# Seven products of sums in place of eight, in the branch projections and the output projection of a hybrid decoder layer

## The chip, the cores and the metric

The kernel runs on one core of a Trainium2 chip. The metric is the device time of one execution in microseconds, the median of three runs. TensorE multiplies float32r operands here, each split into a high and a low part, so every product of matrices is made of three matmuls: high by high, high by low and low by high.

## The reference, cut to what matters

A layer with two parallel branches works on 2048 prompt tokens and 8 sample tokens, with D_MODEL = 1024:

```python
xn = rmsnorm(x, norm_w)
proj = xn @ w_in                      # q k v i f o z_m b c x_c z_c g_m g_c, 10,248 columns
h, C1, n1, m1 = mlstm_chunkwise(q, k, v, ig, lf, ...)
h = h * rsqrt(mean(h * h) + EPS) * head_norm_w
y_m = (h * sigmoid(o_pre) * silu(z_m)) @ w_proj_m
cv, conv1 = short_conv(c_g * x_c, conv0, conv_w)
y_c = (silu(z_c) * b_g * cv) @ w_proj_c
mix = sigmoid(g_m) * y_m + sigmoid(g_c) * y_c
out = x + mix @ w_out
y = rmsnorm(out, final_norm_w)
```

The three products with `w_proj_m`, `w_proj_c` and `w_out` (1024 x 1024 each) are what the change is about.

## The kernel before

The kernel has four phases, one after another, with a barrier of all engines between them.

Phase A norms the input and computes the `v` columns.

Phase B is the input projection for the other columns. It goes over the tokens in three passes of 688, 688 and 680. In a pass it takes 36 pairs of weight column blocks (128 columns each); 18 bodies of two pairs make up the first pass, called `qk` (2), `oz` (4), `conv` (8) and `gates` (4) by what they compute. For each pair the four quarters of the problem (two halves of K by two halves of the tokens by two column blocks) are computed with seven products of sums in the place of eight plain ones, by Winograd's scheme (seven products, fifteen sums). VectorE (DVE) makes the sums of the weights in pass 0 (`sums`), SyncE (SP) stores them to `w_ops_d` and later passes load them. ScalarE (ACT) makes the high part of each operand (`w_high`), DVE the low part (`w_low`), and DVE adds the products up as they leave PSUM (`step`). In passes 1 and 2 the recurrence of the mLSTM is computed between the products. `body` in each engine's program is one such body; all engines go through them in the same order, and each engine's queue is in order. SP issues all DMAs: in a body it loads the weights of the pairs two and three ahead (`load_w`), and stores finished rows (`store_rows`) and sums (`store_w`). GpSimd (POOL) does little: the sums of the x operands at the turn of a pass (`x_sums`, `x_difference`, `x_late`) and small powers.

Phase C computes the branch projections plainly. It keeps `w_proj_m` and `w_proj_c`, split in high and low, in SBUF (`RH`, `RL`) and goes over 7 tiles of TN = 294 tokens; for each of two branches and 8 output blocks it issues 8 x 3 matmuls of 294 columns (line 2017). DVE multiplies the PSUM results by the gates (`gate_m`, `gate_c`) and a tile of `mix` is stored to DRAM.

Phase D loads `w_out` over the same buffers and goes over 17 tiles of 128 tokens (the last has 8); each takes 2 x 8 x 3 matmuls of 512 columns with the activations as the stationary operand (line 2207). DVE adds the residual, ACT squares, POOL takes the power, DVE scales by `final_norm_w`, and SP stores.

Of the kernel before, what the change touches and what calls it, by code (L numbers as in the profile page):

```python
# [28 lines left out]
P = 128  # L29
# [20 lines left out]
TN = 294  # L50
NTC = 7
TP = TN * NTC
# [31 lines left out]

class Shared:
# [3 lines left out]
def build(nc, inputs, outputs):  # L89
# [4 lines left out]
    with top:  # L94
# [9 lines left out]
        g.w_ops_d = dram("w_ops_d", NPP, P, 4 * 4 * P)  # L104
        g.qT_d = dram("qT_d", NH, P, TP)
# [14 lines left out]
        g.stage_in = {name: [top.enter_context(nc.semaphore(f"{name}_in{j}")) for j in range(2)] for name in ("wc", "mix")}  # L120
        g.mix_out = top.enter_context(nc.semaphore("mix_out"))
# [3 lines left out]
        g.act_in = top.enter_context(nc.semaphore("act_in"))  # L125
# [3 lines left out]
        g.XS = sbuf(nc, early, "x_quarters", [P, 5, 4, TQ])  # L129
        g.LH = sbuf(nc, early, "w_hi", [P, NOP, 4, P], F32R)  # L130
        g.LL = sbuf(nc, early, "w_lo", [P, NOP, 4, P], F32R)
        g.X0H = sbuf(nc, early, "x_hi0", [P, 4, TQ], F32R)
# [3 lines left out]
        g.v_stored = [early.enter_context(nc.semaphore(f"a_v_stored{j}")) for j in range(2)]  # L136
        with early:
            phase_a(nc, g)
            phase_b(nc, g)
        g.RH = sbuf(nc, top, "RH", [P, KB, 2 * D], F32R)  # L140
        g.RL = sbuf(nc, top, "RL", [P, KB, 2 * D], F32R)
        g.A0 = [sbuf(nc, top, f"first_act_{n}", [P, KB, TN], F32R) for n in ("hi", "lo")]
        g.m_hi, g.m_ready = top.enter_context(nc.semaphore("m_hi")), top.enter_context(nc.semaphore("m_ready"))
        g.RHf = g.RH[:, :, :].bitcast(F32)
        phase_c(nc, g)
        phase_d(nc, g)

# [469 lines left out]
def phase_b(nc, g):  # L617
# [54 lines left out]
    BANK = (0, 1, 2, 3, 0, 2, 3)  # L672
# [16 lines left out]
    const_in, const_set, pads = sem("const_in"), sem("const_set"), sem("pads")  # L689
    kq_in, m_in, v_in, gate_in, hg_out = sem("kq_in"), sem("m_in"), sem("v_in"), sem("gate_in"), sem("hg_out")  # L690
# [36 lines left out]
    def over_segments(eng, body):  # L727
# [11 lines left out]
        return before  # L739

# [66 lines left out]
    with nc.Block() as block:  # L807
# [3 lines left out]
        def _(sp):  # L811
# [40 lines left out]

            def store_w(pair, par):
# [133 lines left out]
            def body(p, s, i, extra, following, before):  # L987
# [19 lines left out]
                if s == "gates" and i == 0 and p < 2:  # L1007
                    load_quarters(p + 1)
# [1237 lines left out]
```

## Time and profile before

| | |
|---|---|
| device time, three runs | 2356.53, 2359.93, 2360.93 us; median 2359.93 |
| span of the profiled execution | 2356.7 us; the page has no other time for it |
| TensorE (PE) busy | 2323.1 us, 99% of the span, 14,643 matmuls |
| VectorE busy | 1488.1 us, 63% |
| ScalarE busy | 948.6 us, 40% |
| GpSimd busy | 77.5 us, 3% |
| DMA | 425.66 MB, mean 181 GB/s |

The profile's line numbers (L1658) are those of the kernel file. A row of the timeline gives the start, the time taken, the engine, the line and the operation, and in square brackets how long the engine had been idle and what released it. Instructions in a row overlap by some 0.08 us on VectorE, so their starts stand closer than their durations. For TensorE a matmul's duration is the time until its result is out; the rate is given by the distance of the starts.

### The profile page before, as it was taken

The page shows a single profiled execution, that of the slowest core. Times are in us where ns is not written, and L with a number is a line of the kernel's source. Part 1 is how long each engine was busy: PE and PEld are TensorE (multiplying, and loading weights), DVE is VectorE, ACT ScalarE, POOL GpSimd, SP SyncE. Part 2 cuts the span into 40 slices and gives each one's busy share as a digit, 9 for nine tenths or more (in the row PEclk, how much of TensorE's full clock was granted, in tenths as well). Part 3 has the DMA queues.
Part 4 walks back from the last instruction along what each step waited for, and adds up shares of the span by engine and source line. Part 5 has one row for each costly group of instructions (what it writes and reads, how often), then busy time and mean ns, then how long its engine had stood idle before and what let it go on. Part 6 is the DMA issues. An engine that isn't in the chain of part 4 may idle for free. (4 is left out here: it accounts for less than half of the span.)

```text
span 2356.7 us, 41040 instructions
## 1 busy us (share of the span) xinstructions
PE 2323.1 (99%) x14643; PEld 2254.8 (96%) x14643; DVE 1488.1 (63%) x2703; ACT 948.6 (40%) x1717; POOL 77.5 (3%) x84
## 2 busy tenths in 40 slices
PE   8999999999999999999999999999999999999998
PEld 8998999999999999999999999999998999998886
DVE  4447788898876687777776677777755333324333
ACT  3224444444454444455655444555554101002121
POOL 0011000000110000000020000000000000000000
PEclk9999999999999999999999999999999999999999
DMA  6665655455775765656765766557567433443442
GB/s 224 209 215 136 199 187 181 157 177 176 232 220 174 232 202 184 191 159 195 240 191 177 235 202 195 188 175 217 176 185 260 156 102 110 138 143 126 138 138 86
DMA packets 424977, 425.66 MB, mean 181 GB/s; under 512 B 32810, under 2 KB 363690, under 8 KB 424870
## 3 DMA queue, kind: packets, MB, share of 16 engines
q1 hardware_dynamic: 424870, 424.25, 56.9%
q8 instruction: 66, 1.08, 0.2%
q14 instruction: 41, 0.34, 0.0%
HBM read 297.36 MB, written 126.85 MB: 180 GB/s over the span
## 5 line engine op out<-in xcount | busy, mean ns | idle before, releaser
L1658 PE MATMUL b_g<-x_hi,w_hi 128*128 128x344 f32 (+1 forms) x3024 | 985.5, 326 | 9.0 <-DVE rows L1333 4.3
L1658 PE MATMUL b_g<-x_lo,w_hi 128*128 128x344 f32 (+1 forms) x3024 | 967.9, 320 | 0.0
L1658 PE MATMUL b_g<-x_hi,w_lo 128*128 128x344 f32 (+1 forms) x3024 | 967.0, 320 | 0.0
L1658 PEld LDWEIGHTS b_g<-x_hi,w_hi 128*128 128x128 f32 x3024 | 569.3, 188 | 16.1 <-DVE rows L1333 4.4
L1658 PEld LDWEIGHTS b_g<-x_lo,w_hi 128*128 128x128 f32 x3024 | 569.3, 188 | 1.7
L1658 PEld LDWEIGHTS b_g<-x_hi,w_lo 128*128 128x128 f32 x3024 | 569.4, 188 | 0.0
L1155 ACT ACTIVATE w_hi<-w_operands 128x512 fp32r<-128x512 f32 x519 | 323.5, 628 | 272.9 <-PE b_g L1658 261.2
L1295 DVE TENSOR_TENSOR w_lo<-w_operands,w_hi 128x512 fp32r<-128x512 f32 x519 | 354.2, 695 | 1.2
L1155 ACT ACTIVATE w_hi<-stages 128x512 fp32r<-128x512 f32 x216 | 134.7, 629 | 138.3 <-PE b_g L1658 119.4
L1295 DVE TENSOR_TENSOR w_lo<-stages,w_hi 128x512 fp32r<-128x512 f32 x216 | 145.6, 684 | 7.7 <-ACT w_hi L1155 6.9
L2017 PE MATMUL c_g<-act_hi,RH 128*128 128x294 f32 x448 | 134.4, 300 | 2.1 <-DVE rows L1948 2.1
L2017 PE MATMUL c_g<-first_act_hi,RH 128*128 128x294 f32 x448 | 134.1, 299 | 1.6 <-DVE RL L1941 1.6
L2017 PE MATMUL c_g<-act_hi,RL 128*128 128x294 f32 x448 | 134.0, 299 | 0.0
L2017 PE MATMUL c_g<-first_act_hi,RL 128*128 128x294 f32 x448 | 133.8, 299 | 0.0
L2017 PE MATMUL c_g<-first_act_lo,RH 128*128 128x294 f32 x448 | 133.7, 299 | 0.0
L2017 PE MATMUL c_g<-act_lo,RH 128*128 128x294 f32 x448 | 133.5, 298 | 0.0
L579 PE MATMUL a_v<-wv_hi,xT_hi 128*128 128x344 f32 (+1 forms) x384 | 124.5, 324 | 4.5 <-DVE wv_lo L481 2.8
L1326 DVE TENSOR_TENSOR part<-part,b_g 128x344 f32<-128x344 f32 (+1 forms) x108 | 55.1, 510 | 112.4 <-PE b_g L1658 112.0
L579 PE MATMUL a_v<-wv_lo,xT_hi 128*128 128x344 f32 (+1 forms) x384 | 122.7, 320 | 0.0
L579 PE MATMUL a_v<-wv_hi,xT_lo 128*128 128x344 f32 (+1 forms) x384 | 122.7, 319 | 0.0
L1335 DVE TENSOR_TENSOR rows<-part,b_g 128x344 f32<-128x344 f32 (+1 forms) x108 | 55.1, 510 | 89.8 <-PE b_g L1658 87.9
L1173 ACT ACTIVATE part<-b_g 128x344 f32<-128x344 f32 (+1 forms) x108 | 49.3, 457 | 143.5 <-PE b_g L1658 143.4
(305 smaller groups left out, 3116.0 us busy)
## 6 DMA issues: line engine op xcount, KB each, us to landing
w_operands<-w_in SPq DMA_DIRECT2D x282, 256.0 KB, 5.2
stages<-w_ops_d SPq DMA_DIRECT2D x36, 768.0 KB, 5.5
w_operands<-w_ops_d SPq DMA_DIRECT2D x34, 768.0 KB, 4.9
stages<-w_in SPq DMA_DIRECT2D x72, 256.0 KB, 3.8
w_operands<-w_ops_d SPq DMA_DIRECT2D x70, 256.0 KB, 6.3
w_ops_d<-w_operands SPq DMA_DIRECT2D x18, 768.0 KB, 3.3
w_ops_d<-stages SPq DMA_DIRECT2D x18, 768.0 KB, 3.4
w_ops_d<-w_operands SPq DMA_DIRECT2D x36, 256.0 KB, 3.9
```

The source lines that it names most:

```text
L579: last = nc.tensor.matmul(V[3 * (i % 2) + j][:n, 0:VC], x[:, k, 0:n], w[:, k, j * VC:(j + 1) * VC], start=(k == 0 and m == 0), stop=(k == ...
L1155: nc.scalar.activation(LH[:, j], operand(g, par, j), ACT.Copy).then_inc(w_hi, 1)
L1173: nc.scalar.activation(P1[:, 0:n], G[0][:, 0:n], ACT.Copy).then_inc(x_free, 1)
L1295: nc.vector.tensor_tensor(LL[:, j], operand(g, par, j), LH[:, j].bitcast(F32), ALU.subtract).then_inc(w_ready, 1)
L1326: nc.vector.tensor_tensor(U2[:, 0:n], P1[:, 0:n], G[1][:, 0:n], ALU.add).then_inc(ev, 1)
L1335: nc.vector.tensor_tensor(ER[:, q, 1, 0:n], U2[:, 0:n], G[2][:, 0:n], ALU.add).then_inc(ev, 1)
L1658: last = nc.tensor.matmul(bank[:, 0:n], w[:, j, k, :], x[:, k, 0:n], start=(j < 4 and k == 0 and m == 0), stop=(k == 3 and m == 2), skip_g ...
L2017: last = nc.tensor.matmul(G[o % NB][:, 0:TN], w[:, k, c0:c0 + P], x[:, k, :], start=(k == 0 and m == 0), stop=(k == KB - 1 and m == 2))
```

## The change

Phases C and D become one phase, `phase_cd`, without a barrier between them, in which both the branch projections and the output projection use the seven-product scheme of phase B.

- **Branches.** Tokens go in 4 groups of 2 x 258 (TN = 258, NG = 4). For each branch, group and pair of output blocks there are 7 products of 4 x 3 matmuls of 258 columns. Two column pairs are interleaved in a unit `u`, so 16 units of 14 products. ACT copies the first and the fifth product of each out of PSUM, DVE adds the other five (`step`), and a gate is one operation over 1032 columns (`gate`).
- **Output.** Tiles of 2 x 128 tokens, 8 of them, each 7 products of 4 x 3 matmuls of 512 columns; the 8 sample rows come last with 48 plain matmuls.
- **Merge of the branches.** `mix_d` gets the first branch's rows by a plain store, and the second branch's by 16 accumulating DMAs that GpSimd issues (`accumulate`).
- **Weights.** The 12 pairs of weight blocks (4 for each matrix) are read in 12 bodies of the first pass of phase B (`block_of`: `oz` 1 to 3, all of `conv`, `gates` 0). GpSimd makes four sums for each (`projection_sum`), and all seven operands are kept in `proj_d` in DRAM. The buffers used (`kT`, `qT`, `MB` and `HB`) are not otherwise in use then. The operands are loaded in phase CD, seven at a time, and split there in high and low by ACT and DVE.
- **head_norm_w** is no longer folded into `w_proj_m` but into the `z` rows: ACT has one more operation of 688 columns for each `oz` row.
- The sums of the activations (`act_sum`) and their splits (`act_high`, `act_low`) are made once for four column pairs. The first group's are made in the last bodies of phase B.

The diff, cut to its core:

```diff
-TN = 294
-NTC = 7
-TP = TN * NTC
+TN = 258
+NG = 4
+TP = 2 * TN * NG
+NU = 4 * NG
...
+            def load_weights(b):
+                if b:
+                    sp.wait_ge(q_out, 16 * NOP * b)
+                w, c0, c1 = weight_block(g, b)
+                w = w[0].rearrange("(k p) n -> p k n", p=P)
+                for place, k0, c in zip(raw_pieces, (0, 0, 4, 4), (c0, c1, c0, c1)):
+                    sp.dma_start(place, w[:, k0:k0 + 4, c:c + P]).then_inc(q_in, 16)
+                for j, k0, c in ((0, 0, c0), (4, 4, c0), (5, 4, c1)):
+                    sp.dma_start(g.proj_d[b, :, j], w[:, k0:k0 + 4, c:c + P]).then_inc(q_out, 16)
+            def store_sums(b):
+                sp.wait_ge(q_set, 4 * (b + 1))
+                for place, j in zip(raw_pieces[1:], (2, 6, 1, 3)):
+                    sp.dma_start(g.proj_d[b, :, j], place).then_inc(q_out, 16)
...
+                if block_of(p, s, i) is not None:
+                    load_weights(block_of(p, s, i))
                 if extra == "dec_inputs":
                     decode_inputs()
                 if extra == "dec_rows":
                     decode_rows()
...
+            def projection_sum(b, at):
+                r0, r1, r2, r3, t = raw_pieces
+                if at == 0:
+                    pool.wait_ge(q_in, 64 * (b + 1))
+                    nc.gpsimd.tensor_tensor(t, r1, r3, ALU.add).then_inc(q_set, 1)
+                elif at == 1:
+                    pool.wait_ge(q_set, 4 * b + 1)
+                    nc.gpsimd.tensor_tensor(r3, t, r0, ALU.subtract).then_inc(q_set, 1)
+                elif at == 2:
+                    nc.gpsimd.tensor_tensor(r1, r0, r1, ALU.subtract).then_inc(q_set, 1)
+                else:
+                    pool.wait_ge(q_set, 4 * b + 2)
+                    nc.gpsimd.tensor_tensor(r2, r2, r3, ALU.subtract).then_inc(q_set, 1)
...
+def act_low(nc, dve, g, s, j):
+    high, low = act_parts(g, s, j)
+    dve.wait_ge(g.x_hi, 7 * s + j + 1)
+    nc.vector.tensor_tensor(low, act_source(g, s, j), high.bitcast(F32), ALU.subtract).then_inc(g.x_ready, 1)
...
+            def accumulate(n):
+                pool.wait_ge(gated, n + 1)
+                pool.dma_start(two_rows(g.mix_d, n), MX[n % 2], accum_op=ALU.add).then_inc(g.acc_out[n % 2], 16)
...
+            for u in range(NU):
+                s = u // 2 + 1
+                for j in range(NOP):
+                    if j == 0 and u:
+                        gate(2 * u - 2)
+                        gate(2 * u - 1)
+                        if u % 2 == 0:
+                            act_low(nc, dve, g, s - 1, NOP - 1)
+                    step(2 * u, j)
+                    step(2 * u + 1, j)
+                    if u == 0 and 1 <= j < 4:
+                        split_low(nc, dve, g, 0, j + 3)
+                        act_low(nc, dve, g, 0, j + 3)
+                        split_low(nc, dve, g, 1, j + 3)
+                    for b, o in behind(u, j):
+                        split_low(nc, dve, g, b, o)
+                    if u % 2 == 0 and j >= 5:
+                        act_sum(nc, dve, g, s, j - 5)
+                    if u % 2 and j:
+                        act_low(nc, dve, g, s, j - 1)
+                        if j < 3:
+                            act_sum(nc, dve, g, s, j + 1)
...
+            def branch_product(n, j):
+                br, t, p = place(n)
+                if t == 0:
+                    pe.wait_ge(g.w_ready, split_count(4 * br + p, j))
+                if p == 0:
+                    pe.wait_ge(g.x_ready, 7 * (n // 4) + j + 1)
+                if n > 1:
+                    bank_free(n - 2, j, copies, parts_made)
+                bank_read(n, j, copies, parts_made)
+                high, low = act_parts(g, n // 4, j)
+                bank = G[4 * (n % 2) + BANK[j]]
+                for k in range(4):
+                    for m, (w, x) in enumerate(((0, high), (0, low), (1, high))):
+                        last = nc.tensor.matmul(bank[:, 0:TN], g.W[:, p, j, w, k, :], x[:, k, :], ...)
```

SyncE's queue in the `oz` bodies of the first pass, before (the loads into `stages` are the weights of the pair three ahead, those into `w_operands` x4 of the pair two ahead; `gate_d` is a finished row, `w_ops_d` the sums of phase B):

```order
L162 DMA w_operands<-w_in 128x4x128 [waits b_w_ops_out0,b_w_ready]
L162 DMA w_operands<-w_in 128x4x128 x3
L863 DMA gate_d<-rows 128x680 [waits b_gate_set]
L865 DMA gate_d<-rows 128x8
L857 DMA w_ops_d<-stages 128x1536 [waits b_w_sums_set]
L858 DMA w_ops_d<-w_operands 128x512
L162 DMA stages<-w_in 128x4x128 [waits b_w_ops_out1,b_w_ready]
```

And the same stretch in the changed kernel:

```order
L207 DMA w_operands<-w_in 128x4x128 [waits b_w_ops_out0,b_w_ready]
L207 DMA w_operands<-w_in 128x4x128 x3
L1044 DMA gate_d<-rows 128x680 [waits b_gate_set]
L1046 DMA gate_d<-rows 128x8
L1038 DMA w_ops_d<-stages 128x1536 [waits b_w_sums_set]
L1039 DMA w_ops_d<-w_operands 128x512
L1025 DMA kT<-w_proj_m 128x4x128 [waits b_q_out]
L1025 DMA qT<-w_proj_m 128x4x128
L1025 DMA neg_max<-w_proj_m 128x4x128
L1025 DMA h<-w_proj_m 128x4x128
L1027 DMA proj_d<-w_proj_m 128x4x128 x3
L207 DMA stages<-w_in 128x4x128 [waits b_w_ops_out1,b_w_ready]
```

Seven DMAs, with a wait for the stores of the block before, stand ahead of the load of the pair three ahead. At the body's end, ahead of the next body's load of the pair two ahead, stand the four stores of sums (`proj_d` from `qT`, `neg_max` and twice `h`), the first of which waits for GpSimd's sums.

GpSimd's queue in the first pass, before: after the constants only loop branches stand ahead of the sums at the turn of the pass.

```order
L1132 AFFINE_SELECT cum_upper<-ones 128x128 [waits b_const_set]
L1134 AFFINE_SELECT mask<-mask 128x128
L736 UNCONDITIONAL_BRANCH
L736 REGISTER_ALU
L736 COMPARE_AND_BRANCH
L736 UNCONDITIONAL_BRANCH
```

In the changed kernel, at the same place, the first loop has the four sums of a block (`h`, `qT`, `kT` and `neg_max` are the borrowed buffers):

```order
L1347 AFFINE_SELECT mask<-mask 128x128
L893 UNCONDITIONAL_BRANCH
L893 ISA
L1309 TENSOR_TENSOR h<-qT,h 128x512 [waits b_q_in]
L1311 ISA
L1312 TENSOR_TENSOR h<-h,kT 128x512 [waits b_q_set]
L1314 TENSOR_TENSOR qT<-kT,qT 128x512
L1316 REGISTER_ALU
L1317 TENSOR_TENSOR neg_max<-neg_max,h 128x512 [waits b_q_set]
```

Each of the four reads two SBUF tensors of 512 columns; they run twelve times in all. VectorE's program in that pass is as before.

VectorE's queue near the start of phase C, before (`RL` are low parts of weights, `act_lo` of activations; `rows` takes results out of PSUM, with the gate):

```order
L1941 SCALAR_TENSOR_TENSOR RL<-stages,head_norm_q,RH 128x1024 [waits c_w_hi]
L1941 SCALAR_TENSOR_TENSOR RL<-act_stage,head_norm_q,RH 128x1024 [waits c_w_hi]
L1935 TENSOR_TENSOR act_lo<-act_stage,act_hi 128x2352 [waits c_a_hi1]
L1944 TENSOR_TENSOR RL<-act_stage,RH 128x1024 [waits c_w_hi]
L1948 SCALAR_TENSOR_TENSOR rows<-tanh_gate,c_g 128x294 [waits last_rows_out1,c_tile_done,last_rows_out0,c_tg_in0]
L1948 SCALAR_TENSOR_TENSOR rows<-tanh_gate,c_g 128x294 [waits c_tile_done] x2
L1944 TENSOR_TENSOR RL<-stages,RH 128x1024 [waits c_w_hi]
L1948 SCALAR_TENSOR_TENSOR rows<-tanh_gate,c_g 128x294 [waits c_tile_done] x3
```

And in the first unit of the new phase (`proj_whole` are weight operands as loaded, `proj_ops` their parts; `c_part` and `rows` take sums out of PSUM):

```order
L319 TENSOR_TENSOR act_lo_b<-x_quarters,act_hi_b 128x1032 [waits xq_hi]
L242 TENSOR_TENSOR proj_ops<-proj_whole_55,proj_ops 128x512 [waits proj_hi]
L242 TENSOR_TENSOR proj_ops<-proj_whole_56,proj_ops 128x512 [waits proj_hi]
L242 TENSOR_TENSOR proj_ops<-proj_whole_57,proj_ops 128x512 [waits proj_hi]
L2303 TENSOR_TENSOR rows<-c_part,c_g 128x258 [waits c_done] x2
L242 TENSOR_TENSOR proj_ops<-proj_whole_56,proj_ops 128x512 [waits proj_hi]
L242 TENSOR_TENSOR proj_ops<-proj_whole_57,proj_ops 128x512 [waits proj_hi]
L273 TENSOR_TENSOR x_quarters<-x_quarters 128x1032 [waits xq_in1]
L2306 TENSOR_TENSOR rows<-c_part,c_g 128x258 [waits c_done] x2
L242 TENSOR_TENSOR proj_ops<-proj_whole_56,proj_ops 128x512 [waits proj_hi]
L242 TENSOR_TENSOR proj_ops<-proj_whole_57,proj_ops 128x512 [waits proj_hi]
L276 TENSOR_TENSOR x_quarters<-x_quarters 128x1032 [waits xq_sum]
```

Here the first sum for the second group of activations (`x_quarters`, waiting for `xq_in1`, its load) stands ahead of the reads of PSUM for the seventh product (L2306) and of later weight parts.

## Rows read from the trace of the kernel before

**Rows 1.** The page: busy time, share of the span, instructions.
```profile
PE 2323.1 (99%) x14643; PEld 2254.8 (96%) x14643; DVE 1488.1 (63%) x2703; ACT 948.6 (40%) x1717; POOL 77.5 (3%) x84
```

**Rows 2.** Stretches: length, then busy us (count) by engine, granted clock, DMA share, GB/s.
```profile
358.73:385.28 26.55, 26.55 (x170) 26.55 (x170) 21.31 (x37) 12.77 (x24) 0.00 (x0) 1.00 0.56 185
518.03:544.58 26.55, 26.55 (x170) 26.55 (x169) 23.62 (x43) 11.67 (x20) 0.00 (x0) 1.00 0.52 171
597.68:624.23 26.55, 26.55 (x170) 26.55 (x169) 20.73 (x36) 12.24 (x21) 1.04 (x1) 1.00 0.84 278
1830.00:2150.00 320.00, 320.00 (x2354) 320.00 (x2353) 108.72 (x173) 35.16 (x21) 0.00 (x0) 1.00 0.39 125
2173.00:2340.00 167.00, 167.00 (x720) 134.62 (x720) 56.86 (x75) 30.55 (x45) 8.13 (x15) 1.00 0.43 132
```

**Rows 3.** TensorE's timeline at the borders of phases C and D, and its last matmul.
```profile
1783.50 2.02 PE L2023 MATMUL c_g<-ident 128*128 128x128 f32 x16 [0.87 <-PEq L807]
1786.42 0.37 PE L2017 MATMUL c_g<-first_act_hi,RH 128*128 128x294 f32 x1 [0.90 <-DVE RL L1941]
...
2156.22 0.29 PE L2017 MATMUL c_g<-act_hi,RL 128*128 128x294 f32 x1
2158.39 0.47 PE L2207 MATMUL d_g<-RH,first_act_hi 128*128 128x512 f32 x1 [1.87 <-PEq L1814]
...
2349.41 0.40 PE L2207 MATMUL d_g<-RH,first_act_lo 128*8 128x512 f32 x1
```

**Rows 4.** TensorE's timeline in phase B: eight records of 128 columns in a row.
```profile
1004.28 1.04 PE L1717 MATMUL b_t<-ident,h 128*128 128x128 f32 x8
1005.07 0.40 PE L1658 MATMUL b_g<-x_hi,w_hi 128*128 128x344 f32 x1
```

**Rows 5.** GpSimd's timeline: sums of 512 and of 1376 columns.
```profile
172.49 1.29 POOL L363 TENSOR_TENSOR w_operands<-w_operands 128x512 f32<-128x512 f32 x1
...
626.81 3.50 POOL L1095 TENSOR_TENSOR x_quarters<-x_quarters 128x1376 f32<-128x1376 f32 x1
697.24 3.17 POOL L1101 TENSOR_TENSOR x_quarters<-x_quarters 128x1376 f32<-128x1376 f32 x1 [66.92 <-DVE x_lo L1316]
```

**Rows 6.** VectorE's timeline at the same times.
```profile
623.03 0.69 DVE L1295 TENSOR_TENSOR w_lo<-w_operands,w_hi 128x512 fp32r<-128x512 f32 x1
626.29 0.99 DVE L1302 TENSOR_TENSOR stages<-stages,w_operands 128x512 f32<-128x512 f32 x1 [2.58 <-DMA w_operands<-w_in]
627.21 0.50 DVE L1337 TENSOR_TENSOR rows<-part,b_g 128x344 f32<-128x344 f32 x1
627.63 3.23 DVE L1295 TENSOR_TENSOR w_lo<-w_operands,w_hi 128x512 fp32r<-128x512 f32 x1
...
695.57 1.59 DVE L1316 TENSOR_TENSOR x_lo<-x_quarters,x_hi 128x1376 fp32r<-128x1376 f32 x1
697.50 4.35 DVE L1316 TENSOR_TENSOR x_lo<-x_quarters,x_hi 128x1376 fp32r<-128x1376 f32 x1
```

**Rows 7.** SyncE's issues in a `conv` body.
```profile
530.21 0.46 SPq L858 DMA_DIRECT2D w_ops_d<-w_operands  x1
534.13 0.38 SPq L162 DMA_DIRECT2D stages<-w_in  x1
534.55 0.51 SPq L162 DMA_DIRECT2D w_operands<-w_in  x1
```

**Rows 8.** SyncE and VectorE in `conv` 2: rows sent through DRAM.
```profile
451.74 0.81 SPq L970 DMA_DIRECT2D qk_rows<-scores  x1
...
458.43 0.44 SPq L977 DMA_DIRECT2D sample_wide<-fir_d  x1
...
462.13 0.23 DVE L1570 TENSOR_TENSOR sample_wide<-sample_wide 128x64 f32<-128x64 f32 x1 [3.40 <-DMA sample_wide<-fir_d]
```

**Rows 9.** DMA issues by tile: count, KB each, median us to landing.
```profile
w_operands<-w_in SPq DMA_DIRECT2D x282, 256.0 KB, 5.2
...
mix_d<-rows SPq DMA_DIRECT2D x7, 1176.0 KB, 6.7
```

More of the change, by code:

```diff
@@ L1113, in body @@
             def body(p, s, i, extra, before):
+                if block_of(p, s, i) is not None:
+                    for at in range(4):
+                        projection_sum(block_of(p, s, i), at)
                 if extra == "chunk":
@@ new lines, in phase_cd @@
+    N = D // 2
+    at = g.places
+    tail = g.XS[:, :, :, :].rearrange("p s k n -> p (s k n)")[:, 20 * TN:26 * TN].rearrange("p (a n) -> p a n", n=TN)
+    TG = [at_place(nc, "tanh_gate", [P, 2, 2 * TN], at["gate"])[:, :, :], tail[:, 0:4].rearrange("p (a h) n -> p a (h n)", a=2)]
+    P1 = [tail[:, 4], tail[:, 5]]
+    parts = at_place(nc, "c_part", [P, 2, TN], at["part"])
+    U2 = [parts[:, 0], parts[:, 1]]
+    rows = g.ER[:, :, :, :].rearrange("p q r n -> p q (r n)")
+    MX = [rows[:, q, 0:4 * TN].rearrange("p (a n) -> p a n", a=2) for q in range(2)]
@@ new lines, in y_stored, with two_rows, row_free, behind @@
+    def y_stored(i):
+        return 16 * (NU // 2 + i // 2 + 1)
+    def two_rows(a, n):
+        _, t, p = place(n)
+        return a.rearrange("(a b) p n -> b p a n", a=2)[p][:, :, t * 2 * TN:(t + 1) * 2 * TN]
+    def row_free(eng, n):
+        if n < 2:
+            eng.wait_ge(g.row_out[n], g.rows_stored[n])
+        elif n - 2 < NU:
+            eng.wait_ge(rows_out[n % 2], 16 * ((n - 2) // 2 + 1))
+        else:
+            eng.wait_ge(g.acc_out[n % 2], 16 * ((n - 2 - NU) // 2 + 1))
+    def behind(u, j):
+        found = split_behind(u, j)
+        return [(2 * found[0] + q, found[1]) for q in range(2)] if found else []
@@ L1914, in _ @@
+            act_high(nc, act, g, 0, 3)
             for br in range(2):
                 row = g.ER[:, 1, br, 0:2 * PASSES[2][1]]
[L1916 to L1925 removed]
@@ new lines, in _ @@
+            pe.wait_ge(sx_set, 3)
+            pe.wait_ge(copied, out_copies(NT2 - 2, 4))
+            pe.wait_ge(ev, out_parts(NT2 - 2, 1))
+            for h, operands in enumerate((((0, 0), (1, 4)), ((0, 3), (2, 5)))):
+                count = 0
+                for a, j in operands:
+                    for k in range(4):
+                        for x, w in ((SH, 0), (SH, 1), (SL, 0)):
+                            last = nc.tensor.matmul(G[h][:NS, :], x[:, a, k, :], g.W[:, :, j, w, k, :],
+                                                    start=(count == 0), stop=(count == 23))
+                            count += 1
```

906 lines of the change are left out of this document (513 added, 393 removed).

## The prediction

> **What bounds the kernel now.** First the busy times of the page [rows 1]: TensorE is busy for 2323.1 of 2356.7 us, so only fewer or shorter matmuls, or fewer gaps between them, can give much. Next the stretches by engine [rows 2]. The reader should divide length by count there. In phase B 170 records (344 columns for nearly all) take 26.55 us, 156.2 ns each. In phase C 2354 matmuls of 294 columns take 320 us, 135.9 ns. In phase D 720 of 512 columns take 167 us, 231.9 ns. TensorE has no gap in these stretches and the granted clock is 1.00, so each is at the rate of TensorE itself. Last the borders [rows 3]: phase C's first TensorE work starts at 1783.50, phase D's at 2158.39, the last matmul ends at 2349.8, and 6.9 us of norm and store follow.
>
> **What the change takes off TensorE.** The branches have 2 x 8 x 7 tiles x 24 = 2688 matmuls of 294 columns now, and 32 x 7 x 12 = 2688 of 258 columns after. The count stays; seven products for eight shows as narrower matmuls (2064 x 7/8 columns and padding). From 344 to 294 columns the spacing falls by 20.3 ns, 0.41 ns a column; from 512 to 344 by 0.45 [rows 2]. For 36 columns fewer than 294 that gives 119.7 to 121.3 ns; I take 121. Sum: 2688 x 0.121 = 325.2 us. The output has 17 x 48 = 816 matmuls of 512 columns now and 8 x 84 + 48 = 720 after: 720 x 0.2319 = 167.0 us.
>
> Now the two phases take 2158.39 - 1783.50 = 374.9 us (with 16 ident records, the waits at the start and the barrier to D) and 2349.8 - 2158.4 = 191.4 us [rows 3]. If the new phase starts at once and never waits, it needs 492.2 in place of 566.3: **74.1 us less**. The end is the same chain for the 8 sample rows, 6.9 us.
>
> **What it adds in the first pass.** Twelve bodies get four GpSimd sums of 512 columns. One takes 1.29 us [rows 5], so 5.2 us a body. They are not free for VectorE. Read [rows 5] and [rows 6] side by side: while GpSimd runs its sum from 626.81 to 630.31, a `w_lo` of VectorE that takes 0.69 otherwise takes 3.23, and ends 0.55 after GpSimd. `x_lo` takes 1.59 alone and 4.35 beside the sum of 697.24. A sum out of PSUM (0.50 at 627.21) isn't held up. So an operation of VectorE with both inputs in SBUF waits for the whole GpSimd sum. The Trainium skill, "SBUF — State Buffer", "Who interferes with whom", says the same as a rule: the two engines take a shared read port by an exclusive lock for the whole instruction. By that rule "sums on GpSimd" would cost VectorE all of its 5.2 us; the trace agrees.
>
> VectorE's room in a body is 26.55 less its busy time [rows 2]: 5.2 us in `oz`, 2.9 in `conv`, 5.8 in `gates`. Of the 5.2 us some part is no loss, since a PSUM read (0.42 from start to start, 627.21 to 627.63) can run under a sum; with one under every second sum 4.3 us are lost. Then `oz` and `gates` still fit, and each of the 8 `conv` bodies is 1.4 us over: 11 us. Bounds: nothing, if TensorE's slack in PSUM banks (a bank is read two products after its result, 3.8 us) hides it; 2.3 x 8 = 18 us, if all 5.2 are lost.
>
> SyncE has seven more issues ahead of the load of the pair three ahead. At 0.42 to 0.55 us each these take 3.7 us; the gap there is 3.5 (530.67 to 534.13) [rows 7]. That is hidden, and so are the four stores at the body's end. The added traffic is 11 x 256 KB = 2.9 MB a body, on top of 171 GB/s x 26.55 us = 4.5 MB: 280 GB/s. The busiest stretch shown moved 278 GB/s at a DMA share of 0.84 [rows 2], without a TensorE gap. So `conv` and `oz` are near the limit but under it; `gates` 0 is that very stretch and goes to 385 GB/s. I put 2 us on it. One place is worse: in `conv` 2, `load_weights` stands ahead of `decode_rows`. Now SyncE goes from 451.74 to 458.43 through it, the broadcast lands at 462.1, and VectorE has already waited 3.40 us [rows 8]. 3.7 us of issues and the queued 1.8 MB (5 to 6 us at 330 GB/s, which is 278 at a share of 0.84 taken to the full [rows 2]) come in front: VectorE waits some 5 us longer. TensorE has to pay most of that, 4 us. Sum for the pass: 11 + 4 + 2 = **17 us**, bounds 3 and 35 (upper: 18, and late weight loads costing up to 2 us a `conv` body with the DMA queue full).
>
> ACT's added operation on `z` rows (688 columns) lies in bodies where ACT is busy for 12.8 of 26.55 us [rows 2]: nothing.
>
> **What it adds in the new phase.** A unit `u` is 168 matmuls, 20.3 us. VectorE's work in it, from start-to-start times: a sum out of PSUM 0.42 at 344 columns, 0.34 at 258 (less 86 columns at 1.05 ns, the slope from 512 to 1376 columns, 0.69 to 1.59 us [rows 6]); a split or sum of 1032 columns 1.15; a weight split 0.60. An even unit has 10 x 0.34 + 2 gates + 1 + 2 x 1.15 = 9.2 us, an odd one 10 x 0.34 + 10 x 1.15 = 14.9. Unit 0 has no gates, but ten weight splits with four activation splits, six weight splits of the next pair and two sums: 3.4 + 9.6 + 4.6 + 2.3 = 19.9. Unit 1 has eight more weight splits, 19.7. Elsewhere it is at most 18. So VectorE is full only for the first two units, and there it stands at the sum that waits for `xq_in1`: that load is issued when the first group is split (some 16 us into the phase), is 2.1 MB behind 4 MB of weights and gates, and lands about 25 us in, 5 to 6 us after VectorE is there. The weight parts for unit 1 behind it then come 1 to 2 us late in three places: **5 us**, bounds 1 and 15. In the output part VectorE has 5 x 0.64 + 7 x 0.60 + 4 x 0.60 + 4 x 1.15 = 14.4 us of 19.5 for a tile: 0.5 us.
>
> The accumulating DMAs (528 KB) have no row. The nearest is a store of 1176 KB with 6.7 us to landing [rows 9], and a load of 256 KB with 5.2; for 528 KB I take 6 to 10. The rows are written again 7.7 us after the second gate, and 5.8 us more pass before TensorE needs that bank. So it costs nothing up to 13 us of latency, and its upper bound is in the rivals.
>
> **Sum**: 2356.7 - 74.1 + 17 + 5.5 = 2305.1. The median of the runs is 3.2 us above the profiled span, so the median after is **2308 us**.
>
> **The rivals.**
> - *The first pass hides it all* (chance 0.22). For it: most of VectorE's delay is under the bank slack, and `conv` has idle of its own. Pass cost 3, new phase 1 to 5: 2359.9 - 74.1 + 4 to 8, 2290 to 2294.
> - *The first pass is paced by VectorE and DMA* (0.15). For it: [rows 6], and 280 GB/s through one queue with 512-byte pieces. Cost 35 to 50 us: 2326 to 2341.
> - *The weight load paces TensorE* (0.04), so that 258 columns go no faster than 294: 40 us dearer, 2348. For it: the weight loader is busy for 320.00 of 320 us in C [rows 2]. Against: its time shrinks with the columns, and eight records of 128 columns start within 0.79 us, 110 ns each or less [rows 4].
> - *Slower than before* (0.05): the accumulating DMA takes so long that ACT and VectorE stand at `row_free`. From 13 us on, each us costs a us in each of 7 units; the 52 us of the sum are eaten at 13 + 7.5, some 20 us latency; at 22 it gives 2371. For it: an accumulation reads and writes DRAM, and GpSimd must write its descriptors. Against: 1176 KB land in 6.7 us.
> - *The seven products don't save*: in the branches the count stays at 2688, and if the rate per column were not kept (a gap at each of 224 + 56 product changes, each with up to four waits, of 0.1 us) it would cost 28 us: 2336 (0.04). Phase B has the same changes with 0 gaps.
>
> **How the numbers follow.** The forecast's own case (2298 to 2324) has 0.50. 80% range: from 2286 (the first rival inside) to 2334 (the upper part of the second outside). Below 0.2% (4.7 us) this kernel's runs can't tell a change. Faster 0.93, same 0.02, slower 0.05.
>
> **What would show it.** Right: matmuls of 258 columns 121 ns apart; no 2 us gap before the 512-column ones; `w_lo` rows of 1.5 to 2 us beside GpSimd's sums and TensorE gaps of 1 to 2 us in the `conv` bodies, a longer one in `conv` 2; a gap or two in units 0 and 1. Wrong: TensorE without gaps in pass 0 (then some 2290), or gaps in every unit from the second branch on, with `row_free` or `acc_out` behind them (then over 2330).

## The result and the profile after

The changed kernel takes **2377.8 us** (four runs, 2374.4 to 2378.8), the kernel before 2360.3 beside it. The ratio is 1.0077, with a 95% interval of 1.0063 to 1.0092: **slower by 0.8%**, where 2% faster was forecast, and far outside the range. The profiled execution took 2374.4, its span is 2372.4 us.

The page of the changed kernel: busy times, and the queue that GpSimd's DMAs use (packets, MB, share).

```profile
PE 2283.7 (96%) x14531; PEld 2209.3 (93%) x14531; DVE 1690.8 (71%) x2947; ACT 1059.2 (45%) x1961; POOL 166.2 (7%) x140
...
q0 software_dynamic: 4352, 8.46, 2.3%
```

Against [rows 1], TensorE is busy for 39 us less and yet the span is 16 us longer: it now idles for 89 us, not 34. The stretches show where. First the kernel before (phase B), then the changed kernel: phase B, branches, output, one `conv` body, and 60 us in the middle of the branches. The columns are those of [rows 2].

```profile
216.00:1782.60 1566.60, 1558.39 (x9833) 1540.06 (x9833) 1180.36 (x2162) 789.13 (x1521) 52.59 (x33) 1.00 0.62 193
```

```profile
217.00:1816.00 1599.00, 1567.18 (x9833) 1542.26 (x9833) 1227.65 (x2171) 810.33 (x1552) 125.22 (x85) 0.99 0.68 213
1818.00:2194.50 376.50, 340.33 (x2688) 337.78 (x2689) 232.44 (x344) 120.10 (x197) 17.19 (x15) 0.95 0.65 185
2195.00:2365.00 170.00, 168.76 (x719) 129.61 (x718) 124.04 (x179) 60.17 (x107) 8.00 (x10) 1.00 0.47 145
...
560.53:588.55 28.02, 27.54 (x170) 26.46 (x168) 27.20 (x43) 11.55 (x21) 5.92 (x4) 1.00 0.84 266
...
1900.00:1960.00 60.00, 60.00 (x502) 60.00 (x501) 37.07 (x52) 15.10 (x23) 0.00 (x0) 1.00 0.48 150
```

The gain is real where nothing waits: 502 matmuls of 258 columns in 60 us are 119.5 ns each. At that rate the branches would take 2688 x 0.1195 = 321 us. They take 376.5: 36 us more in which TensorE is idle, and 19 more in which it is busy but slow (mean granted clock 0.95). The output takes 170, as forecast to 3 us. Phase B is 32 us longer, some 25 of them in its first pass (run 7 has the rows for this).

**The gaps of the branches.** TensorE's timeline has pauses of 3.75, 3.12, 1.22, 5.30, 4.80 and 7.24 us in units 9 to 15, nearly one in each unit. The timeline around the last one, of GpSimd, VectorE, ACT and TensorE:

```profile
2171.61 1.20 POOL L2185 DMA_DIRECT2D mix_d<-rows  x1 [19.53 <-DVE rows L2312]
...
2181.36 0.42 DVE L2300 TENSOR_TENSOR rows<-rows,c_g 128x258 f32<-128x258 f32 x1 [1.36 <-DMA mix_d<-rows]
...
2181.57 1.22 POOL L2185 DMA_DIRECT2D mix_d<-rows  x1 [8.76 <-issue]
...
2191.29 0.39 ACT L2222 ACTIVATE rows<-c_g 128x258 f32<-128x258 f32 x1 [7.19 <-DMA mix_d<-rows]
2191.33 0.42 DVE L2300 TENSOR_TENSOR rows<-rows,c_g 128x258 f32<-128x258 f32 x1 [9.55 <-DMA mix_d<-rows]
...
2191.81 0.58 PE L2458 MATMUL c_g<-act_hi_b,proj_ops 128*128 128x258 f32 x1 [7.24 <-DVE rows L2300]
...
2193.91 0.42 PE L2458 MATMUL c_g<-act_hi_b,proj_ops 128*128 128x258 f32 x1
2194.12 0.42 PE L2458 MATMUL c_g<-act_lo_b,proj_ops 128*128 128x258 f32 x1
```

Read from the end: TensorE waits for VectorE's step, that for the buffer of the second gated row, and that for its accumulating DMA. The two rows of a unit are gated 1.2 us apart, but GpSimd issues the second DMA 10 us after the first. It lands 9.6 us after that, 19.6 us after the first issue and 18.8 after its own row was gated. The last two rows show the other cost: behind the pause the matmuls stand 0.21 us apart, not 0.12, and the next row of the windows gives the granted clock there.

```profile
2192.40:2194.50 2.10, 2.10 (x11) 2.10 (x11) 2.10 (x4) 2.10 (x5) 0.00 (x0) 0.50 0.00 0
```

0.50 is the level of 1.2 GHz. And GpSimd's second issue comes at 2181.57, just as the first DMA has landed and released VectorE (2181.36). The line L2185 as a group: who waited for it (us, times), and its time to landing.

```profile
  DVE rows L2300: 71.0, 13
  ACT rows L2222: 63.6, 9
...
DMA to landing us min/median/max: 6.0/8.4/10.2
```

**The gaps of the first pass.** `conv` 2 and the first `gates` body, SyncE's issues first.

```profile
454.52 0.94 SPq L1025 DMA_DIRECT2D kT<-w_proj_c  x1
...
461.04 0.86 SPq L1151 DMA_DIRECT2D qk_rows<-scores  x1
...
470.72 0.23 DVE L1792 TENSOR_TENSOR sample_wide<-sample_wide 128x64 f32<-128x64 f32 x1 [9.19 <-DMA sample_wide<-fir_d]
...
471.63 0.62 PE L1889 MATMUL b_g<-x_hi,w_hi 128*128 128x344 f32 x1 [7.33 <-DVE rows L1555]
...
628.97 3.95 SPq L1133 DMA_DIRECT2D x_quarters<-xT_d  x4
632.96 1.10 SPq L1025 DMA_DIRECT2D kT<-w_out  x1
634.11 2.47 SPq L1025 DMA_DIRECT2D qT<-w_out  x1
...
643.94 0.58 SPq L207 DMA_DIRECT2D stages<-w_in  x1
...
650.93 3.26 DVE L1524 TENSOR_TENSOR stages<-stages,w_operands 128x512 f32<-128x512 f32 x1 [11.02 <-DMA w_operands<-w_in]
...
654.67 0.66 PE L1889 MATMUL b_g<-x_hi,w_hi 128*128 128x344 f32 x1 [8.31 <-DVE rows L1559]
```

The seven issues of a block take SyncE 6.5 us in `conv` 2 and 11.0 in the first `gates` body (632.96 to 643.94), not 3.7. VectorE waits 9.2 us for the broadcast (3.40 in [rows 8]) and 11.0 for weights of phase B. Both times TensorE pauses, and runs at the half level behind it.

### The profile page after: what moved, and what is told of

The parts are those of the page before. It is cut to its first block, busy times and chain, and to the rows that moved or that the text cites. A ratio compares the mean times of both kernels' runs of the same rounds, so it can differ in the third digit from the quotient of the medians.

```text
span 2372.4 us, 41561 instructions
## 1 busy us (share of the span) xinstructions
PE 2283.7 (96%) x14531; PEld 2209.3 (93%) x14531; DVE 1690.8 (71%) x2947; ACT 1059.2 (45%) x1961; POOL 166.2 (7%) x140
## 4 chain that ended last, share of the span: by engine, by line
PE 59%; DVE 12%; DMA 8%; issue 6%; SPq 3%; ACT 1%; DVEq 0%; POOL 0%; ACTq 0%; POOLq 0%
PE b_g L1889 44%; PE c_g L2458 5%; PE c_g L2482 5%; DMA mix_d<-rows 3%; DMA w_operands<-w_ops_d 2%; DVE w_lo L1517 2%; PE b_n L1943 1%; PE b_n L1944 1%; PE b_s L1942 1%; DVE proj_ops L242 1%; DMA proj_whole<-proj_d 1%; DMA new_C_sample<-gate 1%; DMA y_prompt<-y 1%; DVE x_lo L1538 1%; DVE act_lo_a L319 1%
## 5 line engine op out<-in xcount | busy, mean ns | idle before, releaser
L1889 PE MATMUL b_g<-x_hi,w_hi 128*128 128x344 f32 (+1 forms) x3024 | 988.4, 327 | 34.2 <-DVE rows L1555 14.5
L1517 DVE TENSOR_TENSOR w_lo<-w_operands,w_hi 128x512 fp32r<-128x512 f32 x519 | 368.8, 723 | 1.2
L2458 PE MATMUL c_g<-act_hi_a,proj_ops 128*128 128x258 f32 x1024 | 195.7, 291 | 8.6 <-DVE proj_ops L242 4.7
L2458 PE MATMUL c_g<-act_hi_b,proj_ops 128*128 128x258 f32 x768 | 149.2, 291 | 29.4 <-DVE rows L2300 26.6
L2458 PEld LDWEIGHTS c_g<-act_hi_a,proj_ops 128*128 128x128 f32 x1024 | 166.3, 197 | 9.6 <-DVE proj_ops L242 7.2
L2458 PEld LDWEIGHTS c_g<-act_hi_b,proj_ops 128*128 128x128 f32 x768 | 124.9, 196 | 31.2 <-DVE rows L2300 24.1
L2458 PE MATMUL c_g<-act_lo_a,proj_ops 128*128 128x258 f32 x512 | 148.3, 290 | 0.0
L2482 PE MATMUL c_g<-proj_ops,act_hi_a 128*128 128x512 f32 x448 | 141.4, 396 | 1.2 <-DVE y L2379 0.9
L313 ACT ACTIVATE act_hi_a<-x_quarters 128x512 fp32r<-128x512 f32 (+1 forms) x88 | 68.9, 786 | 95.8 <-PE c_g L2482 50.2
L2458 PE MATMUL c_g<-act_lo_b,proj_ops 128*128 128x258 f32 x384 | 111.2, 290 | 0.0
```

What stands on the lines that cost most here:

```text
L313: nc.scalar.activation(act_parts(g, s, j)[0], act_source(g, s, j), ACT.Copy).then_inc(g.x_hi, 1)
L1517: nc.vector.tensor_tensor(LL[:, j], operand(g, par, j), LH[:, j].bitcast(F32), ALU.subtract).then_inc(w_ready, 1)
L1889: last = nc.tensor.matmul(bank[:, 0:n], w[:, j, k, :], x[:, k, 0:n], start=(j < 4 and k == 0 and m == 0), stop=(k == 3 and m == 2), skip_g ...
L2458: last = nc.tensor.matmul(bank[:, 0:TN], g.W[:, p, j, w, k, :], x[:, k, :], start=(j < 4 and k == 0 and m == 0), stop=(k == 3 and m == 2), ...
L2482: last = nc.tensor.matmul(bank[:, :], x[:, k, :], g.W[:, :, j, w, k, :], start=(j < 4 and k == 0 and m == 0), stop=(k == 3 and m == 2), sk ...
```

## The experiments

Each ran beside the kernel before; "won" is the change of the ratio against that of the changed kernel (1.0077), times 2360 us.

**1. More descriptor space** (with the small tiles moved to make room):

```diff
-    nc = bacc.Bacc("TRN2", ..., dynamic_dma_scratch_size=1024)
+    nc = bacc.Bacc("TRN2", ..., dynamic_dma_scratch_size=3072)
```

> The computation is the changed kernel's; GpSimd's space for DMA descriptors is 3072 bytes in place of 1024, and small tiles moved elsewhere to make room. In the changed kernel the second accumulating DMA of a unit is issued 9.0 to 10.6 us after the first, each time 0.3 us after the first has landed, and the second's rows are free only some 18 us after their gate. Theory A (the descriptor space holds one of these DMAs, so the second waits for the first to land): the second issue follows within 3 us of the first, both rows are free 8 to 13 us after their gate, TensorE's gaps in units 8 to 15 (26 us, and 34 us of half clock behind them) shrink to under 6 us, and the time is 2374 - 35 = 2339 us (2330 to 2348). Theory B (GpSimd needs 9 us to write the descriptors of one, or an accumulation is slow in itself): the distance stays at 9 to 10 us and the time within 4 us of the changed kernel's.

2359.6 us, ratio 1.0004 (0.9995 to 1.0014): 17 us won. GpSimd's timeline and the landing time of its DMAs:

```profile
2159.04 2.44 POOL L2186 DMA_DIRECT2D mix_d<-rows  x2 [28.64 <-DVE rows L2313]
...
DMA to landing us min/median/max: 6.6/10.0/13.6
```

The second issue now follows the first at once, in all eight units. The serial issue of theory A is shown. Its sum isn't: the time is 12 us over the top of its range. Two DMAs in flight land later (10.0 us in the median, up to 13.6), and the rows still cost pauses of 0.5 to 2.2 us in units 9 to 15, 7.1 us together. And there is a gap of 7.2 us at 2150.6, with 10.2 us at the half level, that isn't the rows':

```profile
2129.89 13.41 SPq L266 DMA_DIRECT2D x_quarters<-mix_d  x8
...
2149.11 1.15 ACT L238 ACTIVATE proj_ops<-proj_whole 128x512 fp32r<-128x512 f32 x2 [23.50 <-DMA proj_whole<-proj_d]
```

ACT's copy of a product stands behind the split of an output weight, and SyncE issues that weight's load only behind 13.4 us of issues for the output's activations.

**2. No accumulation:** the second branch's rows go out through SyncE like the first's.

```diff
-                sp.dma_start(two_rows(g.mix_d, n), MX[n % 2]).then_inc(rows_out[n % 2], 16)
+                out = rows_out[n % 2] if n < NU else g.acc_out[n % 2]
+                sp.dma_start(two_rows(g.mix_d, n), MX[n % 2]).then_inc(out, 16)
```

> The second branch's rows are stored plainly by SyncE over the first branch's, without accumulation: the sum of the branches is left out. The bytes stored are the same, GpSimd issues no DMA. If the gaps of units 8 to 15 come from the accumulating DMAs (their serial issue or their slowness), they vanish as in units 1 to 6, where the same rows go out by plain stores that land in 8 to 9 us: 2374 - 40 = 2334 us (2326 to 2342). If they come from something else in those units (the loads of the third pair of weight blocks, the activations, VectorE's own work), the gaps stay and the time is within 5 us of 2374. Against the run with the larger descriptor space: equal within 5 us if only the serial issue cost time; lower by over 5 us if accumulation itself is slow too.

2344.2 us, 0.9938 (0.9921 to 0.9954): 33 us won, 2 us over the range expected; the branches take 341.4 us for 376.5. The gaps of units 8 to 15 are gone but one of 2.5 us, at the start of unit 15; those of units 1 and 7 stay. It is 15 us under run 1, so to issue the accumulating DMAs together won only half of what taking them away won. About half of the 15 are run 1's pauses for rows (7.1 us); most of the rest is its gap behind the output weights, 7.2 us there and 2.5 here, and the half level behind it. Whether accumulation as such makes that gap longer was not tried.

**3. Four buffers for the gated rows**, accumulation and descriptor space as in the changed kernel:

```diff
-    MX = [rows[:, q, 0:4 * TN].rearrange("p (a n) -> p a n", a=2) for q in range(2)]
+    MX = [r.rearrange("p (a n) -> p a n", a=2) for r in
+          (S_flat[:, 0:4 * TN], S_flat[:, 4 * TN:8 * TN], rows[:, 0, 0:4 * TN], rows[:, 1, 0:4 * TN])]
...
+        elif n - 4 < NU:
+            eng.wait_ge(mix_out[n % 4][0], mix_out[n % 4][1] + 16 * (n // 4))
+        else:
+            eng.wait_ge(g.acc_out[n % 4], 16 * ((n - 4 - NU) // 4 + 1))
```

> The computation is the changed kernel's, with the descriptor space of 1024 bytes; the gated rows of the new phase take turns in four buffers in place of two (the two new ones lie in the staging buffer, which is idle there), so that the rows of a unit are written again two units later. Theory (the rows come free too late: 18 us after the gate against a need after about 13): with a full unit of 20 us more, no wait for a store or an accumulating DMA is left in ACT or VectorE in units 2 to 15, the gaps of 26 us in units 8 to 15, the half clock behind them (34 us, worth 17) and the gap of 1.1 to 3 us at unit 8 go: 2378 - 40 = 2338 us (2330 to 2345). The run with more descriptor space gave 2360: if this one is equal to it, the waits for rows were not what cost the rest, and contention with the accumulating DMAs is.

2346.0 us, 0.9943 (0.9927 to 0.996): 32 us won, one us over the range expected. The branches:

```profile
1818.40:2162.90 344.50, 330.45 (x2688) 329.19 (x2689) 232.45 (x343) 118.45 (x193) 17.09 (x14) 0.98 0.69 197
```

Nobody waits for `mix_d` from a gated row any more, though GpSimd's issues are still serial. The slow DMA costs nothing once its buffer has a unit more. The largest gaps left aren't the rows': 4.7 us in unit 1, and 4.9 at 2140.6, where ACT's copy of a product stands behind splits of late output weights as in run 1.

**4. The sums of activations in unit 1 in place of unit 0:**

```diff
-                    if u % 2 == 0 and j >= 5:
+                    if u % 2 == 0 and u and j >= 5:
                         act_sum(nc, dve, g, s, j - 5)
+                    if u == 1 and j == 0:
+                        act_sum(nc, dve, g, s, 0)
+                        act_sum(nc, dve, g, s, 1)
```

> In the changed kernel with only the first two sums of the second group's activations moved in VectorE's queue from unit 0 (products 5 and 6) to unit 1 (behind the steps of product 0). There VectorE stands 9.1 us for the load of the x quarters, and TensorE 4.7 us at 1849.1 with 6.8 us of half clock behind it. Theory (the sum stands in front of weight parts whose operands are there): the gap shrinks to 1 to 2 us and the half clock goes: 5 to 7 us less than the changed kernel, 2371 to 2373. Rival (the weights of the second pair are late themselves, 16 loads of 256 KB behind 4.7 us of issues): less than 2 us.

2374.4 us, 1.0058 (1.0041 to 1.0075): 4.5 us won, by the medians 3.4; the interval overlaps the changed kernel's, so by the time alone this gain isn't sure. In the trace the gap of 4.66 us at 1849 is gone, and the half level behind it; two gaps of 1.1 us (at 1859.9 and 1864.2) stand in the place of that one and one of 0.8. The 3.4 us of half level that this profile has here lie at the start of the phase, behind the border. Nearer the first theory.

**5. The first pass without GpSimd's block sums:**

```diff
-                    nc.gpsimd.tensor_tensor(t, r1, r3, ALU.add).then_inc(q_set, 1)
+                    pool.sem_inc(q_set, 1)
```

and so for the other three.

> GpSimd's four sums of each weight block are left out in the first pass (the loaded quarters are stored in their place, so the results of the branches and of the output are wrong); all DMAs stay. In the changed kernel the first pass is 32 us longer than before: gaps of 7.3 us at 471.6 and 8.3 us at 654.7 with 17 us of half clock behind them, four gaps of 0.6 to 1.0 us at 434 to 449, and about 0.7 us in each 25 us of the other conv bodies. Theory of the prediction (VectorE is held up by GpSimd's sums): the small gaps go, 11 us less by my term, and the two large ones stay: about 2366 us. Theory of the queue (SyncE's issues and late landings cost the time): under 4 us less, 2371 to 2376.

2362.1 us, 1.0011 (1.0001 to 1.0022): 16 us won. Phase B takes 1587.0 us, 12 less than in the changed kernel. The small gaps went and the two large ones stayed (5.9 and 4.5 us in place of 7.3 and 8.3, so that 5 us of the gain are theirs): the theory of VectorE held up by GpSimd.

**6. The loads moved in SyncE's queue:**

```diff
+                if extra == "dec_rows":
+                    decode_rows()
                 if block_of(p, s, i) is not None:
                     load_weights(block_of(p, s, i))
-                if extra == "dec_rows":
-                    decode_rows()
...
-        ... (s == "gates" and not (isinstance(i, int) and i == 0)) ...
+        ... (s == "gates" and not (isinstance(i, int) and i == 2)) ...
```

> Only the order of SyncE's queue in the first pass changes: in the third conv body the rows that go through DRAM are sent ahead of the weight block, not behind it, and the last weight block is read in the third gates body, not in the first. Theory of the queue (the seven issues stand ahead of what VectorE waits for, and the first gates body has no room for them beside the x quarters): the gaps at 471.6 (7.3 us) and 654.7 (8.3 us) shrink to 1 us each and the half clock behind them goes (17 us at half, worth 8.5): 20 to 24 us less, 2350 to 2356. Theory of contention (the traffic of the blocks itself delays the broadcasts and loads): the gaps stay at 4 to 8 us, and at most 8 us are won.

2364.3 us, 1.0022 (1.0009 to 1.0034): 13 us won, phase B 1584.9. SyncE and VectorE in `conv` 2:

```profile
456.53 0.34 SPq L1157 DMA_DIRECT2D sample_wide<-fir_d  x1
...
460.39 0.23 DVE L1792 TENSOR_TENSOR sample_wide<-sample_wide 128x64 f32<-128x64 f32 x1 [1.38 <-DMA sample_wide<-fir_d]
```

VectorE waits 1.4 us for the broadcast, not 9.2; the gaps shrink to 1.6 and 1.1 us and phase B has no half level left. The mechanism is that of the queue. I had priced it too high by some 8 us. The granted clock falls inside the gap, so part of the 17 us at half level lay where TensorE stood anyway: what followed the two gaps was 4.1 and 5.3 us, worth 4.7, not 8.5. And there is a new gap of 1.6 us at 698.3, behind GpSimd's sums for the next pass, which now start after the block's.

**7. Runs 5 and 6 together:**

> Two edits in the changed kernel together: the loads moved in the first pass, and GpSimd's block sums left out (the loaded quarters are stored in their place, so the branches and the output are wrong). Phase B takes 1566.3 us before, 1598.5 in the changed kernel, 1586.7 without the sums, 1584.6 with the moved loads. If the two are separate causes, the gains add (11.8 + 13.9) and phase B takes 1573 us, 7 above before: 2378 - 26 = 2352 us. If they are the same loss seen twice, it stays at 1582 to 1585 and the time at 2361 to 2364. What is left above 1566 is the cost of the added DMAs alone (2.9 MB a body in 12 bodies).

2348.0 us, 0.9955 (0.9938 to 0.9972). Phase B takes 1572.0 us (1573 expected): two separate causes. A `conv` body in it:

```profile
518.03:544.58 26.55, 26.55 (x170) 26.55 (x169) 23.60 (x43) 11.67 (x21) 0.00 (x0) 1.00 0.89 283
```

That is the length of [rows 2] again to the hundredth, with 283 GB/s in place of 171: the traffic alone costs a `conv` body nothing.

Nor are the 5.4 us that remain over the kernel before the DMAs'. TensorE has the same small pause some 18 us into the second pass in the kernel before, the changed kernel and this run, in this order:

```profile
714.99 0.40 PE L1658 MATMUL b_g<-x_hi,w_hi 128*128 128x344 f32 x1 [0.44 <-DVE part L1329]
```

```profile
741.87 0.39 PE L1889 MATMUL b_g<-x_hi,w_hi 128*128 128x344 f32 x1 [0.41 <-DVE part L1551]
```

```profile
713.87 0.39 PE L1889 MATMUL b_g<-x_hi,w_hi 128*128 128x344 f32 x1 [0.41 <-DVE part L1551]
```

Counted from the start of phase B (215.96, 217.38 and 217.58) these are 499.0, 524.5 and 496.3 us. So the changed kernel loses 25.5 us up to there and 7 behind it; this run is 2.7 us ahead there, and loses 8 behind it, where no block is read. In the `oz` bodies of those passes TensorE's pauses sum to 8.2 us for 3.8 before. One of them, VectorE before and in this run:

```profile
845.00 0.87 DVE L1356 SCALAR_TENSOR_TENSOR rows<-z_tanh,rows 128x688 f32<-128x688 f32 x1 [0.65 <-ACT z_tanh L1199]
```

```profile
846.27 0.87 DVE L1578 SCALAR_TENSOR_TENSOR rows<-z_tanh,rows 128x688 f32<-128x688 f32 x1 [1.40 <-ACT rows L1413]
```

L1413 is ACT's added operation on the `z` rows. VectorE waits for it with the reads of PSUM queued behind. No run takes it out, so that it causes these pauses is read from the rows and not shown by an experiment. The rest of the 8 us stays open.

**8. The block sums on VectorE**, behind products 1 to 4 of the body's second half:

```diff
+                        if q and 1 <= j < 5 and block_of(p, s, i) is not None:
+                            projection_sum(block_of(p, s, i), j - 1)
```

> In the changed kernel with the four sums of each weight block on VectorE in place of GpSimd, in the second half of the body, one behind each of products 1 to 4. Leaving the sums out won 15 us. One takes VectorE 0.69 us, 2.8 us a body, against 5.2 us of GpSimd beside which VectorE's operations with both inputs in SBUF stand. Theory of the lock (the cost is the time in which GpSimd's sums hold VectorE up): 2.8 us fit into the oz and gates bodies and nearly into the conv bodies (23.6 of 26.55 us busy before): 6 to 12 us less than the changed kernel, 2366 to 2372. Rival (VectorE's order, not its load, sets the loss: the sums wait for loads that land late and everything behind them waits): equal or up to 15 us more, 2378 to 2393.

2383.3 us, 1.0099 (1.0082 to 1.0116): 5 us lost. My theory missed here, the rival holds. A `conv` body, and VectorE's first block sum in it:

```profile
526.88:555.80 28.92, 28.35 (x168) 28.06 (x168) 25.67 (x47) 11.36 (x20) 0.00 (x0) 0.94 0.81 254
...
554.63 0.69 DVE L1521 TENSOR_TENSOR h<-qT,h 128x512 f32<-128x512 f32 x1 [2.61 <-DMA h<-w_out]
```

This body has 3.4 us at the half level; the next one, at the full clock, takes 28.9 us too. VectorE is less busy than with GpSimd's sums beside it (25.67 for 27.20 us), but stands 2.1 to 3.5 us for the block's loads in the `conv` bodies from the third on, and 12.2 us in the first `gates` body, with everything else queued behind. Whether sums placed a body later would win was not tried.

**9. Runs 3, 4 and 6 in one kernel:**

> Three of the edits in one: four buffers for the gated rows, the moved loads of the first pass (rows through DRAM ahead of the block in the third conv body, the last block in the third gates body), and the two sums of activations moved to unit 1. If the three losses are separate, the gains add: 40 + 13 + 6 us less than the changed kernel, 2378 - 59 = 2319 us (2312 to 2328), 1.7% under the kernel before. If the waits only shift (later transfers come closer together), half of it: 2345.

2327.2 us, 0.9857 (0.984 to 0.9873): 52 us won. Alone the three won 32, 4.5 and 13, 49 together. The gains add.

**10. The output's activations behind its weights** in SyncE's queue of unit 14:

```diff
-                if u == NU - 2:
-                    load_mix(0)
-                    load_mix(1)
                 if u in (6, 7, 14, 15):
                     ...
+                if u == NU - 2:
+                    load_mix(0)
+                    load_mix(1)
```

> The combined kernel, and in SyncE's queue of unit 14 the loads of the first two output tiles' activations (eight loads in 512-byte pieces, 13 us of issues) behind the loads of the first pair of output weights, in place of ahead of them. In the combined kernel TensorE stands 5.0 us in that unit at 2125.5, where ACT's copy of a product is behind splits of those weights, with 6.8 us of half clock behind. Theory (the weights are late behind the activations in one queue): the gap goes to under 1.5 us, 6 to 8 us less than 2327: 2320 us. Rival (the activations are then late for the first output tile): the gap moves to the border at 2148 and nothing is won, 2325 to 2332.

2326.2 us, 0.9858 (0.9842 to 0.9875): nothing. The gap of 5.0 us went, and gaps of 1.4 and 3.2 us came where VectorE waits 9.7 us for the activations. The rival: SyncE's one queue is full in that unit, whatever stands first.

**11. Also no block in the third `conv` body**, one more in the second `gates` body:

```diff
-        return {"oz": lambda: i - 1, "conv": lambda: i + 3, "gates": lambda: 11}[s]()
+        if s == "conv" and isinstance(i, int) and i == 2:
+            return None
+        return {"oz": lambda: i - 1, "conv": lambda: i + 3 if isinstance(i, int) and i < 2 else i + 2, "gates": lambda: i + 9}[s]()
```

> The kernel of the run before, and in the first pass no weight block in the third conv body (whose rows go through DRAM); the blocks behind it move on by one body, and the second gates body takes one. Seven conv bodies in place of eight have GpSimd sums. Theory: a conv body with a block takes 28.05 us in place of 26.55, and the third one has gaps of 0.6 to 1.5 us more; the gates bodies have 5.8 us of room for VectorE: 2 to 5 us less than the run before. Rival (the gates bodies have no room for the traffic): equal or up to 5 us more.

2322.4 us, 0.9853 (0.9834 to 0.9873). **The fastest: 1.5% faster than the kernel before, 2.2% faster than the changed one.** Against run 10 the medians differ by 3.8 us but the intervals overlap; in the profiles phase B is 5.4 us shorter (1581.3 for 1586.7). Its output part and its page:

```profile
2138.90:2309.20 170.30, 168.63 (x722) 129.42 (x720) 124.93 (x181) 62.44 (x111) 8.00 (x10) 1.00 0.50 153
```

```profile
PE 2268.4 (98%) x14531; PEld 2196.9 (95%) x14531; DVE 1693.2 (73%) x2947; ACT 1060.2 (46%) x1961; POOL 167.9 (7%) x140
```

## Why the prediction was wrong

The sum gave a span of 2305.1; it is 2372.4, 67.3 over. By stretch: phase A 1.4 (no edit there; it differs by up to 5 us between the profiles of these kernels), phase B 15.4 (8.5 in the first pass, which costs 25.5 and not 17, and 7 in the other two, for which I had nothing), the border 1.1, the branches 46.3, the output 3.2.

- **The gain was right.** 258 columns take 119.5 ns (121 forecast), 512 as before. The rivals of the weight load and of the seven products are both out: 60 us pass without a gap.
- **The step that failed is "So it costs nothing up to 13 us of latency"**, with 6 to 10 us for the accumulating DMA. The latency of one was right: 6.0 to 10.2 us, median 8.4, measured. What I did not ask is what stands ahead of it on its own engine. Each unit issues two, one after the other, and the second isn't issued until the first has landed (run 1 shows that this is the descriptor space). From the first issue to the second's landing it is 15.0 to 19.6 us; counted from the second row's gate, as the 13 were, it is 14.5 to 18.8. My own rival's rule, a us in each unit for each us over 13, gives 25 us from these, and the pauses that VectorE's wait for a row ended in units 9 to 15 sum to 25.4. With the half level behind them the rows cost 32 (run 3). I gave that rival 0.05 because I read its condition off one DMA's latency; its sign, gaps in the units of the second branch behind the accumulating DMAs and a time over 2330, is what came. The Trainium skill, "DMA: Bandwidth & Descriptors", "Anatomy of one DMA — SWDGE (gpsimd) path", fits 2.0 us plus the bytes at 436 GB/s for one DMA on the GpSimd path, as an estimate 3.2 us for these 516 KB. The trace disagrees: the fastest of these accumulating DMAs, beside other traffic, took 6.0.
- **The clock was in no term.** With the pauses of 7.3 and 8.3 us in phase B and of 4.7, 3.8, 3.1, 5.3, 4.8 and 7.2 in the branches came stretches of 3.4 to 10.2 us at the level of 1.2 GHz, which reached 4 to 9 us past the pause. In the branches that adds 19 us to 36 us of gaps, in phase B some 5. The kernel before had two such stretches of 3.4 us, at the borders of its phases, and I left them out.
- **GpSimd's lock was right and right in size.** 11 us for eight `conv` bodies; a body takes 28.0 for 26.55, and phase B without the sums is 12 us shorter (run 5), or 13 where the loads are moved (run 7 against run 6). TensorE's gaps in these bodies were of 0.3 to 1.0 us, shorter than the 1 to 2 that I had named as the sign.
- **"SyncE's issues are hidden" failed at two places.** The four us for `conv` 2 and two for the first `gates` body were 14 together (run 6). The term was seven issues at 0.42 to 0.55 us; with the queue full they take up to 2.5 us each. My rival of the pass paced by VectorE and DMA (cost 35 to 50) isn't it: the pass cost 25.5, and the bandwidth in its reason is out (run 7).
- **"Nothing" for ACT's added operation was too little.** I gave it none because ACT has idle time in an `oz` body. But VectorE waits for the row that it writes, and the `oz` bodies of the second and third pass have 4.4 us more of pauses (run 7's rows; argued, not tried).
- **New phase, 5 us:** unit 1 has gaps of 4.7 and 0.8 us and 6.8 us at half level, behind VectorE's wait of 9.1 us in its work for unit 0; run 4 gets back 3.4 to 4.5. Right in the wait and near in size.

So the two largest misses, terms that I held for small and bounded (rows, queue), were where an in-order queue was asked for more than one thing at once.

## What to carry to other kernels

When a transfer's latency is weighed against the time until its buffer is needed, count all transfers that its engine issues in that time, in order, and ask whether the second may start before the first has landed; then give the buffer a turn more where memory allows, which here won nearly as much as taking the slow transfer away. Price an issue on a queue by the rows where that queue is full, not where it is idle. An operation added to an engine with idle time isn't free if another engine waits for its result in order: look at that wait. And a pause of TensorE can cost more than its length, as those of 3.1 to 8.3 us did here: look at the granted clock behind it.

## What the runs showed of the hardware

- With 1024 bytes of descriptor space GpSimd issues its second accumulating DMA of 516 KB (the prediction's 528 KB, in thousands of bytes) about 0.3 us after the first has landed (in each of the seven units before the last; in the first of them issued at 2020.6, landed 8.7 us later, the second issued at 2029.6); with 3072 bytes 1.2 us after the first's issue.
- Two in flight land after 10.0 us in the median, not 8.4.
- SyncE's issues of 256 KB took 1.1 to 2.5 us behind four loads of x quarters (`gates` 0), 0.5 to 1.7 in `conv` 2 and some 0.5 in the kernel before.
- Behind a pause of 7.24 us TensorE ran at 0.50 of its clock, 0.21 us between 258-column matmuls. The pauses of 1.22 and 1.98 us in the branches, and of 2.05 at the border, had no half level behind them; that of 3.12 had.
- 283 GB/s at a DMA share of 0.89 beside a TensorE without a gap.
